# Two hybrid transformer blocks: in both token mixers each engine takes its work in an order of its own

## The chip, the cores and the metric

The kernel is one launch on one core of a Trainium2 chip. The metric is device time in microseconds (us) of that launch, as the median of three runs, on which nothing of the host counts. Engines are named as in the profile: PE (TensorE, matmuls), DVE (VectorE), ACT (ScalarE), POOL (GpSimd), SP (SyncE, which only issues the transfers of the weights).

## The reference

Two blocks of two layers each run one after the other on x of 256 tokens by 1024 features, in fp32.

```python
def first_block(x, c, ...):                       # twice
    mod = (silu(c) @ ada_w[l] + ada_b[l]).reshape(b_, 3, 3, D_MODEL)
    y = swiglu(modulate(x, ...), ffn_w13[l, 0], ffn_w2[l, 0])      # 1024 -> 2*2816 -> 1024
    x = layer_norm(ALPHA * x + 0.5 * (1 + gate) * y, ...)
    y = token_mixer(modulate(x, ...), w_in[l], w_out[l], ...)
    x = layer_norm(ALPHA * x + (1 + gate) * y, ...)
    y = swiglu(modulate(x, ...), ffn_w13[l, 1], ffn_w2[l, 1])
    x = layer_norm(ALPHA * x + 0.5 * (1 + gate) * y, ...)

def token_mixer(h, w_in, w_out, ...):
    # h @ w_in, then three kinds of heads of 64 features, then @ w_out
    oa = gated_delta_rule(l2norm(q), l2norm(k), v, g, beta)        # 6 heads, chunks of 64
    oa = oa * rsqrt(mean(oa * oa) + eps) * gdn_norm * silu(z)
    ob = moba_attention(q, k, v)                                   # 4 heads
    hc = mlstm_chunkwise(q, k, v, i_pre, logf)                     # 6 heads
    hc = (hc*sigmoid(o) - mean) * rsqrt(var + eps) * mlstm_norm
    return concatenate([oa, ob, hc]) @ w_out

def hybrid_layer(x, mem, ...):                    # the second block, twice
    proj = x @ w_in                                                # 4608 columns
    da_o = rms_norm(diff_attention(dq, dk, dv, lam)) * (1 - lam_init)
    hg_o = rms_norm(hgrn2_chunk_scan(forward) + hgrn2_chunk_scan(backward)) * silu(gate)
    mx_o = memory_attention(q, mem @ w_mem_kv)
    x = layer_norm(ALPHA * x + concatenate([da_o, hg_o, mx_o]) @ w_out)
    u = conv3(x @ w_up); x = layer_norm(ALPHA * x + (silu(gate) * val) @ w_down)
```

## The kernel before

**Stages.** The work runs as stages one after the other: per layer of the first block a gated feed-forward, mixer 1, a second feed-forward; per layer of the second block mixer 2 and a feed-forward with a convolution. Each stage multiplies the activations by weights that stream once from memory.

**Weights.** A matrix comes in chunks of 128 x 2048 fp32. SP issues a chunk's transfer into a ring of four buffers W. ACT casts it to the high part h (`Feed.hi`, L564), DVE subtracts to get the low part l (`Feed.lo`, L579), each into one of three buffers. A chunk's cast waits until PE has done with the matrix three before it (`released`). The same call of `Feed.lo` also does pending sums for the modulation vectors (L596). An fp32 product is three matmuls: h times high, l times high, h times low.

**Tiles.** In a mixer PE goes through 32 (mixer 1) or 36 (mixer 2) tiles. A tile is 24 matmuls (L683 to L685, or L696 to L698) into one of two banks in turn. Tile t therefore waits until tile t-2 has been emptied, by ACT (L2176 and near it; L3042 to L3062) or DVE (the causal convolution of mixer 1, L2236).

**Tasks.** Beside the tiles the mixers have tasks, each written for each engine as a generator that yields after a piece. Mixer 1: r (rows of gates and norms, 8 pieces), g (gated delta rule, 49), b (MoBA, 10), m (mLSTM, 13). In g the pieces 17 to 40 are six levels of a triangular inverse by doubling; in each PE multiplies (L1657, L1659: product U; L1675, L1677: product V), ACT copies U (L1855, L1857), DVE subtracts V (L1795). Pieces 41 to 45 form u and the output, 46 to 48 the norm (squares on ACT L1876, sums L1812 on DVE, the root on POOL L1903, products L1816 and L1820), 49 the transposes on PE (L1565) with the split into high and low parts (ACT L1573, DVE L1581 and L1583). m7 is the output product of mLSTM (L2033, L2034), m8 to m12 its norm, m13 its transposes. b10 is MoBA's last split (L1982). Mixer 2: h (HGRN, 43 pieces; h10, 14, 18, 22, 26, 30 and 31 are the products of its levels, L2379, before them the exponentials on ACT, L2610, products on DVE and repeated rows on POOL), d (diff attention, 17; d17 the transposes), e (memory attention, 6; on PE scores L2915, transposes L2924, sums L2932).

**Closing chunks.** The output projection takes 128x512 matmuls (L711 to L713). A first part of it is placed among the last pieces: `out(c)`, 24 matmuls each, two in mixer 1 and four in mixer 2. The rest, the tail, follows them all. In mixer 2 the first two closing chunks read the output of d, the other two that of h, the tail that of e. In mixer 1 the first two read g, the tail the rest.

**What sets the order.** There is one list for each mixer (ORDER1, ORDER2), made from AFTER and AFTER2: after tile n come the pieces named there. PE, DVE and ACT all play that list (`play1`, `play2`). The next chunk's cast and subtraction have no entry: they are done inside `tile`, at the first tile of a chunk, and inside `out`. POOL and SP have their own fixed code. Each engine does its instructions strictly in its order; semaphores make one wait for another.

Of the kernel before, what the change touches and what calls it, by code (L numbers as in the profile page):

```python
# [2323 lines left out]

AFTER2 = ["", "", "", "", "h", "h", "h", "", "h", "h", "h", "hh", "hh", "hh", "hh", "hh", "hh", "hh", "hh", "hhd", "hhd", "hh", "hhd", "hd",
          "hd", "hd", "h", "hd", "hd", "hd", "hd", "hd", "hd", "d", "hd", "hd"]


def order2():
    out = []  # L2330
    for t in range(36):
        out.append(("tile", MIX2[t // 2], t % 2))
        out += [(x,) for x in AFTER2[t]]
    out += [("e",), ("d",), ("e",), ("d",), ("h",), ("e",), ("out", 0), ("e",), ("out", 1), ("e",), ("out", 2), ("e",), ("out", 3)]
    return out


ORDER2 = order2()


def play2(tile, out, **tasks):
    for x in ORDER2:
        if x[0] == "tile":
            tile(x[1], x[2])
        elif x[0] == "out":
            out(x[1])
        else:
            next(tasks[x[0]], None)
    for t in tasks.values():
        for _ in t:  # L2350
            assert False

# [724 lines left out]
def dve_mix2(k, v, s, feed):  # L3077
    l = STAGES[s][1]
    cs = downs(s)
    bounds = dve_bounds(k, v)  # L3080

    def tile(n, j):
        m = FIRST["win2", l, n]
        feed.lo(m + 1 + j)

    def out(c):
        feed.lo(cs[c] + 2)
        if l == 0 and c in (1, 2):
# [144 lines left out]
```

## Time and profile before

| | us |
|---|---|
| median of three runs | 2339.38 (2336.34 to 2340.5) |
| the profiled execution's own time | 2344.83 |
| its span in the profile | 2343.0 |
| PE busy in the span | 2096.9 (89%) |
| DVE, ACT, POOL busy | 1642.7 (70%), 1090.5 (47%), 329.3 (14%) |

The profiled execution is 5.45 us above the median of the runs. The page gives the granted clock of TensorE too, in tenths of full speed: it is 9 or more nearly all along, with some slices of 8 where a mixer ends. The mean is 0.943. Mixer 1 of layer 0 lies at 286 to 560 us, mixer 2 of its layer 0 at 1410 to 1690, mixer 2 of layer 1 at 1893 to 2140; each stretch holds the layer norm at its end.

### The profile page before, as it was taken

Reading aid. Unit: us, or ns where it says so; the run is one execution under the profiler, and the core shown is the slowest. Engines: PE = TensorE matmul, PEld = TensorE weight load, DVE = VectorE, ACT = ScalarE, POOL = GpSimd, SP = SyncE. Lnnn points to the kernel's source line nnn. Section 1 sums busy time; section 2 is a strip of 40 time slices with the busy share of each in tenths; the row PEclk is TensorE's granted clock in tenths of the full one; section 3 lists DMA queues with packets and bytes.
Section 4 is the critical chain, followed back from the end, with each engine's and each line's share of the span. In section 5 each row is a group of like instructions: output and inputs, shape, how many; then the busy total and the mean of one; then the engine's idle time right before and its main releaser. Section 6 shows DMA issues by size and latency. Waiting matters only on the chain.

```text
span 2343.0 us, 35483 instructions
## 1 busy us (share of the span) xinstructions
PE 2096.9 (89%) x14804; PEld 1944.4 (83%) x14804; DVE 1642.7 (70%) x2189; ACT 1090.5 (47%) x1543; POOL 329.3 (14%) x261
## 2 busy tenths in 40 slices
PE   6999889978999999889979996887899988978998
PEld 6999778877997998778969985886799887967996
DVE  6777777548777866776557556975688579657874
ACT  3443463434433543553345434654556465545652
POOL 0000113103000200303012002710110036002000
PEclk9999999989999999999989997998999989978999
DMA  9877642114777667432125653332344543313552
GB/s 365 326 273 303 224 165 107 42 67 181 285 286 283 226 251 276 162 135 85 58 93 189 226 205 138 135 108 73 114 174 182 200 144 125 111 70 144 180 186 102
DMA packets 59791, 409.97 MB, mean 175 GB/s; under 512 B 6832, under 2 KB 6832, under 8 KB 12912
## 3 DMA queue, kind: packets, MB, share of 16 engines
q1 hardware_dynamic: 53424, 384.85, 44.3%
q0 software_dynamic: 5920, 22.43, 2.5%
q8 instruction: 118, 1.93, 0.3%
q10 hardware_dynamic: 288, 0.42, 0.0%
q14 instruction: 41, 0.34, 0.0%
HBM read 404.53 MB, written 3.15 MB: 174 GB/s over the span
## 4 chain that ended last, share of the span: by engine, by line
PE 68%; DVE 20%; ACT 6%; issue 3%; DMA 2%; POOL 2%; DVEq 0%; POOLq 0%; SPq 0%; ACTq 0%
PE ps L683 12%; PE ps L685 11%; PE ps L684 11%; PE ps L711 6%; PE ps L713 6%; PE ps L712 6%; DVE l L579 6%; PE ps L1677 2%; PE ps L696 2%; ACT h L564 2%; PE ps L698 1%; PE ps L697 1%; PE ps L1659 1%; DVE acc L596 1%; DVE gq L2236 1%
## 5 line engine op out<-in xcount | busy, mean ns | idle before, releaser
L579 DVE TENSOR_TENSOR l<-w,h 128x2048 fp32r<-128x2048 f32 (+1 forms) x296 | 689.8, 2334 | 230.7 <-ACT h L564 230.1
L683 PE MATMUL ps<-xh,h 128*128 128x256 f32 x2688 | 780.5, 290 | 50.6 <-DVE xl L862 8.5
L684 PE MATMUL ps<-xl,h 128*128 128x256 f32 x2688 | 765.8, 285 | 0.0
L685 PE MATMUL ps<-xh,l 128*128 128x256 f32 x2688 | 765.3, 285 | 0.0
L564 ACT CAST h<-w 128x2048 fp32r<-128x2048 f32 (+1 forms) x296 | 558.6, 1893 | 302.8 <-PE ps L713 157.1
L683 PEld LDWEIGHTS ps<-xh,h 128*128 128x128 f32 x2688 | 521.3, 194 | 68.9 <-issue 26.6
L684 PEld LDWEIGHTS ps<-xl,h 128*128 128x128 f32 x2688 | 521.1, 194 | 1.9 <-issue 1.9
L685 PEld LDWEIGHTS ps<-xh,l 128*128 128x128 f32 x2688 | 520.9, 194 | 0.0
L711 PE MATMUL ps<-h,hh 128*128 128x512 f32 x528 | 207.2, 392 | 0.0
L713 PE MATMUL ps<-h,hl 128*128 128x512 f32 x528 | 205.5, 389 | 0.0
L712 PE MATMUL ps<-l,hh 128*128 128x512 f32 x528 | 205.4, 389 | 0.0
L904 POOL DMA_DIRECT2D GB<-in_vec x20 | 11.4, 572 | 1176.0 <-DVE ab L806 570.7
L596 DVE SCALAR_TENSOR_TENSOR acc<-w,sc,acc 128x1024 f32<-128x1024 f32 x126 | 167.7, 1331 | 2.8
L696 PE MATMUL ps<-h,xh 128*128 128x256 f32 (+1 forms) x512 | 152.5, 298 | 7.6 <-ACT dqk L3048 6.5
L697 PE MATMUL ps<-l,xh 128*128 128x256 f32 (+1 forms) x512 | 146.5, 286 | 0.0
L698 PE MATMUL ps<-h,xl 128*128 128x256 f32 (+1 forms) x512 | 146.3, 286 | 0.0
L1116 DVE TENSOR_TENSOR hl<-hf,hh 128x256 fp32r<-128x256 f32 x132 | 69.6, 529 | 82.4 <-ACT hh L1111 81.9
L713 PEld LDWEIGHTS ps<-h,hl 128*128 128x128 f32 x528 | 99.1, 188 | 20.8
L712 PEld LDWEIGHTS ps<-l,hh 128*128 128x128 f32 x528 | 99.2, 188 | 20.6 <-issue 0.5
L711 PEld LDWEIGHTS ps<-h,hh 128*128 128x128 f32 x528 | 99.2, 188 | 20.4 <-issue 0.5
L696 PEld LDWEIGHTS ps<-h,xh 128*128 128x128 f32 x512 | 101.4, 198 | 14.7 <-issue 11.6
L697 PEld LDWEIGHTS ps<-l,xh 128*128 128x128 f32 x512 | 101.3, 198 | 0.0
(412 smaller groups left out, 3061.6 us busy)
## 6 DMA issues: line engine op xcount, KB each, us to landing
w<-in_stream SPq DMA_DIRECT2D x362, 1024.0 KB, 4.9
GB<-in_vec POOLq DMA_DIRECT2D x20, 512.0 KB, 6.0
gate<-in_vec POOLq DMA_DIRECT2D x6, 512.0 KB, 4.1
w<-in_stream SPq DMA_DIRECT2D x6, 512.0 KB, 3.8
cst<-in_cst POOLq DMA_DIRECT2D x1, 1160.0 KB, 16.1
memf<-in_memT SPq DMA_DIRECT2D x1, 1024.0 KB, 8.5
xf<-in_xT POOLq DMA_DIRECT2D x1, 1024.0 KB, 9.7
kv<-mk POOLq DMA_DIRECT2D x2, 512.0 KB, 7.1
```

Source lines behind the costliest of these rows:

```text
L564: e.copy(k.H[m % NH][:, 0:z], k.W[n % NW][:, 0:z]).then_inc(k.hi_done, 1)
L579: e.tensor_tensor(k.L[m % NH][:, 0:z], k.W[n % NW][:, 0:z], k.H[m % NH][:, 0:z], SUB).then_inc(k.lo_done, 1)
L596: e.scalar_tensor_tensor(out=A[:, :], in0=W[:, i, :], scalar=k.SC[:, r:r + 1], in1=A[:, :], op0=MUL, op1=ADD).then_inc(k.ada_sum, 1)
L683: p.matmul(P[:, 0:T], H[:, r, o], xh[:, r, :], start=r == 0, stop=False)
L684: p.matmul(P[:, 0:T], H[:, r, o], xl[:, r, :], start=False, stop=False)
L685: i = p.matmul(P[:, 0:T], L[:, r, o], xh[:, r, :], start=False, stop=r == 7)
L696: p.matmul(P[:, 0:n], xh[:, r, o], H[:, r, :], start=r == 0, stop=False)
L697: p.matmul(P[:, 0:n], xh[:, r, o], L[:, r, :], start=False, stop=False)
L698: i = p.matmul(P[:, 0:n], xl[:, r, o], H[:, r, :], start=False, stop=r == 7)
L711: p.matmul(P[:, :], hh[:, f, o], H[:, i, s], start=b, stop=False)
L712: p.matmul(P[:, :], hh[:, f, o], L[:, i, s], start=False, stop=False)
L713: x = p.matmul(P[:, :], hl[:, f, o], H[:, i, s], start=False, stop=e)
```

## The change

The two lists and the functions that played them go. In their place stand six strings, one for each of PE, DVE and ACT in each mixer. A letter is an entry: t a tile, r g b m and h d e the next piece of that task, o a closing chunk (PE only), w one call for the next chunk (`feed.hi` on ACT, `feed.lo` on DVE). The number of pieces, tiles and chunks is what it was. So the cast and the subtraction of a chunk no longer belong to a tile. Two bookkeeping pieces of block 2 (`act_bounds`, `dve_bounds`) go with the chunks that they went with. On DVE of mixer 2, t does nothing. The wait of the gated delta rule's first piece on PE becomes that for both halves of the gate rows, where it was for one. ACT has 2 table loads fewer (41 for 43), one in front of L1541 in each mixer 1. All other instructions are the same, and POOL's and SP's order is unchanged.

Cut to its core (the strings of one mixer; two of the functions that play them):

```diff
-AFTER = ["r", "r", "r", "r", "rr", "r", "r", "g", "g", "gg", "", "gg", "g", "gb", "ggb", "ggb", "ggb", "ggb", "gggb", "gggb", "gggb", "ggb",
-         "gggm", "ggm", "gggm", "ggm", "gggm", "ggm", "gm", "gm", "gm", "gm"]
...
-def play1(tile, out, **tasks):
-    for x in ORDER1:
-        if x[0] == "tile":
-            tile(x[1], x[2])
-        elif x[0] == "out":
-            out(x[1])
-        else:
-            next(tasks[x[0]], None)
+ORDER1 = dict(
+    pe=("t t t t trrrrrrr t tg trg tg t t tg tgggg t t tgbbgg tggb tbgbgg tgggb t tbggggg tgggggg tbbm tmg tm tggggggggg tm tgmg tg tg "
+        "tmg tgmgggoommbmmmm"),
...
+def interleave(order, **parts):
+
+    for x in order.replace(" ", ""):
+        if x in parts:
+            next(parts[x])
...
+def more(f, feed, n):
+
+    for _ in range(n):
+        f(feed.m)
+        yield
...
-    yield from pe_decays(k, p, l, 0, lambda g: GBANK["dk", g], gp, gv, ga, k.rv(l, "RB"))
+    yield from pe_decays(k, p, l, 0, lambda g: GBANK["dk", g], gp, gv, ga, k.rv(l, "RB", 1))
...
     def tile(n, j):
         m = FIRST["win", l, n]
-        if j == 0:
-            feed.hi(m + 2)
...
-        if j == 0:
-            feed.lo(m + 1)
...
-        if j == 0:
-            feed.lo(m + 2)
...
-    play2(tile, out, h=dve_hgrn(k, v, l), d=dve_diff(k, v, l), e=dve_memory(k, v, l))
+    interleave(ORDER2["dve"], w=more(ahead, feed, ORDER2["dve"].count("w")), h=dve_hgrn(k, v, l), d=dve_diff(k, v, l), e=dve_memory(k, v, l))
```

**DVE, end of mixer 1, layer 0, before.** `hc`, `s`, `msq` belong to m, `os`, `ms`, `zs` to g, `l` is a chunk's low part.

```order
L579 TENSOR_TENSOR l_22_70<-w_16_64,h_19_67 128x2048
L2080 TENSOR_TENSOR hc_142<-hc_142,so_106 128x384 x2
L2083 TENSOR_REDUCE s_115<-hc_142 128x6 x2
L2086 TENSOR_SCALAR s_115<-s_115 128x6 x2
L2089 TENSOR_TENSOR hc_142<-hc_142,s_115 128x384 x2
L1812 TENSOR_REDUCE ms_113<-gsq_137 128x6 x2
L2094 TENSOR_REDUCE s_115<-msq_143 128x6 x2
L1816 TENSOR_TENSOR os_136<-os_136,ms_113 128x384 x2
L1820 TENSOR_TENSOR os_136<-os_136,zs_105 128x384 x2
L1982 TENSOR_TENSOR mixl_74<-mo_111,mixh_73 128x256 x2
L2098 TENSOR_TENSOR hc_142<-hc_142,s_115 128x384 x2
```

The same place after:

```order
L579 TENSOR_TENSOR l_22_70<-w_16_64,h_19_67 128x2048
L2060 SCALAR_TENSOR_TENSOR Dk_92_140<-ps,Dk_92_140 128x384 x2
L1819 TENSOR_REDUCE ms_113<-gsq_137 128x6 x2
L1823 TENSOR_TENSOR os_136<-os_136,ms_113 128x384 x2
L1827 TENSOR_TENSOR os_136<-os_136,zs_105 128x384 x2
L1588 TENSOR_SCALAR gtmp_139<-ps,cols_50 128x256
L1590 TENSOR_TENSOR mixl_74<-gtmp_139,mixh_73 128x256
L1588 TENSOR_SCALAR gtmp_139<-ps,cols_50 128x256
L1590 TENSOR_TENSOR mixl_74<-gtmp_139,mixh_73 128x256
L1588 TENSOR_SCALAR gtmp_139<-ps,cols_50 128x256
L1590 TENSOR_TENSOR mixl_74<-gtmp_139,mixh_73 128x256
L2069 TENSOR_SCALAR s_115<-ps 128x6 x2
```

The norm of g (now L1819 to L1827) and its splits stand in one run, and m's come behind them; before, m's first steps stood ahead of g's and the two were mixed. The split of b10 (L1982) has gone further back.

In the same mixer PE's string has `tggggggggg` for tile 26: the nine pieces g32 to g40, products V of the fourth level to V of the sixth, stand with no tile between them. Before, they stood in groups of one to three with tiles 24 to 27 between them.

**ACT, start of mixer 2, layer 0, before.** `K` are HGRN's gates, `qs` its queries, `h` a chunk's high part.

```order
L3044 COPY K_97_145<-ps 128x256
L564 CAST h_18_66<-w_16_64 128x2048
L3044 COPY K_97_145<-ps 128x256 x2
L3059 ACT_TABLE_LOAD
L3059 ACTIVATE K_97_145<-K_97_145 128x1024
L564 CAST h_19_67<-w_13_61 128x2048
L3042 COPY qs_144<-ps 128x256
```

After:

```order
L564 CAST h_18_66<-w_16_64 128x2048
L3028 COPY K_97_145<-ps 128x256 x2
L3043 ACT_TABLE_LOAD
L3043 ACTIVATE K_97_145<-K_97_145 128x1024
L564 CAST h_19_67<-w_13_61 128x2048
L564 CAST h_17_65<-w_14_62 128x2048
L3026 COPY qs_144<-ps 128x256 x2
```

A chunk's cast moved ahead of the copies that empty two tiles, and two casts (for the 5th and 6th w of the mixer) now stand one behind the other before the next copy.

**PE, end of mixer 2, layer 0, before.** `epp`, `epT`, `xq`, `mk`, `mmv` belong to e, `do` to d, `ho` to h; L711 begins the first closing chunk.

```order
L2915 MATMUL ps<-mk_176,xq_151 128x256 x2
L2924 MATMUL ps<-cst_49,epp_178 128x128 x4
L2915 MATMUL ps<-mk_176,xq_151 128x256 x2
L1565 MATMUL ps<-cst_49,do_173 128x128 x8
L1565 MATMUL ps<-cst_49,ho_186 128x128 x8
L2932 MATMUL ps<-epT_179,mmv_177 128x256 x2
L2924 MATMUL ps<-cst_49,epp_178 128x128 x4
L2915 MATMUL ps<-mk_176,xq_151 128x256 x2
L711 MATMUL ps<-h_19_67,mixh_119_167 128x512
```

The same place after:

```order
L2901 MATMUL ps<-mk_176,xq_151 128x256 x2
L1572 MATMUL ps<-cst_49,do_173 128x128 x8
L1572 MATMUL ps<-cst_49,ho_186 128x128 x8
L711 MATMUL ps<-h_19_67,mixh_119_167 128x512
L712 MATMUL ps<-l_22_70,mixh_119_167 128x512
L713 MATMUL ps<-h_19_67,mixl_120_168 128x512
```

PE behind the fourth closing chunk of that mixer, after, up to the tail (L711):

```order
L2918 MATMUL ps<-epT_179,mmv_177 128x256 x2
L2910 MATMUL ps<-cst_49,epp_178 128x128 x4
L2901 MATMUL ps<-mk_176,xq_151 128x256 x2
L2918 MATMUL ps<-epT_179,mmv_177 128x256 x2
L2910 MATMUL ps<-cst_49,epp_178 128x128 x4
L2918 MATMUL ps<-epT_179,mmv_177 128x256 x2
L711 MATMUL ps<-h_17_65,mixh_119_167 128x512
```

The transposes of e (now L2910) no longer stand ahead of those of d and h (now L1572); three pieces of e come together behind the last closing chunk, where before each had a closing chunk behind it.

## Rows read from the trace of the kernel before

**Rows 1.** Windows: stretch, length, PE, PEld, DVE, ACT, POOL busy, PEclk, DMA share, GB/s.

```profile
286.00:560.00 274.00, 234.50 (x1724) 215.19 (x1723) 179.76 (x320) 119.81 (x201) 51.69 (x47) 0.93 0.28 101
...
1410.00:1690.00 280.00, 224.30 (x1509) 203.09 (x1508) 202.07 (x310) 147.32 (x245) 72.08 (x56) 0.88 0.32 114
1893.00:2140.00 247.00, 210.06 (x1452) 192.06 (x1451) 176.95 (x252) 134.93 (x213) 64.98 (x44) 0.90 0.31 112
```

**Rows 2.** Windows over the end of mixer 1 and of mixer 2, layer 0.

```profile
504.00:532.00 28.00, 17.13 (x64) 13.29 (x65) 15.54 (x26) 11.30 (x18) 5.54 (x4) 0.76 0.13 40
1613.00:1669.00 56.00, 41.50 (x164) 31.28 (x164) 32.01 (x73) 21.08 (x43) 2.11 (x3) 0.79 0.22 77
```

**Rows 3.** Waits of PE, 286 to 562: us in total, times, longest.

```profile
PE ps L1565 <- DVE os L1820: 8.9, 1, 8.9
...
PE ps L683 <- DVE gq L2236: 2.4, 3, 1.5
PE ps L1554 <- DVE AT L1752: 2.2, 1, 2.2
PE ps L1599 <- ACT rs L1834: 2.2, 1, 2.2
...
PE ps L1675 <- ACT Ub L1857: 1.7, 1, 1.7
```

**Rows 4.** DVE lines by form, 370 to 470: busy, mean ns, idle before.

```profile
L1795 DVE TENSOR_TENSOR Xb<-Xb,ps 128x384 f32<-128x384 f32 x20 | 10.9, 547 | 2.4 <-PE ps L1677 1.9
```

**Rows 5.** Timeline at the end of mixer 1: start us, us, instruction, [idle before].

```profile
485.77 1.50 PE L2034 MATMUL ps<-vx,Dk 128*128 128x65 f32 x12
...
489.57 0.39 PE L2034 MATMUL ps<-vx,Dk 128*128 128x65 f32 x2
...
500.92 0.48 ACT L1872 COPY os<-ps 128x384 f32<-128x384 f32 x1 [2.20 <-PE ps L1717]
...
504.10 1.28 ACT L2209 ACT_TABLE_LOAD   x1
...
506.68 1.01 DVE L1812 TENSOR_REDUCE ms<-gsq 128x6 f32<-128x384 f32 x2 [3.82 <-ACT gsq L1876]
...
508.08 2.31 POOL L1903 TENSOR_TENSOR ms<-ms,cst 128x12 f32<-128x12 f32 x1
...
512.54 1.09 PE L1565 MATMUL ps<-cst,os 128*128 128x128 f32 x4 [8.86 <-DVE os L1820]
...
531.18 0.39 PE L711 MATMUL ps<-h,mixh 128*128 128x512 f32 x1
```

**Rows 6.** Waits of PE, 1410 to 1690.

```profile
PE ps L2924 <- DVE epp L2957: 8.6, 3, 7.2
PE ps L2379 <- DVE A L2496: 6.7, 3, 5.0
```

**Rows 7.** Timeline of ACT at the start of mixer 2.

```profile
1462.09 0.39 ACT L3046 ACTIVATE K<-ps 128x256 f32<-128x256 f32 x1 [2.44 <-PE ps L685]
1462.37 1.91 ACT L564 CAST h<-w 128x2048 fp32r<-128x2048 f32 x1
1464.92 0.37 ACT L3044 COPY K<-ps 128x256 f32<-128x256 f32 x1 [0.64 <-PE ps L685]
```

**Rows 8.** DVE and POOL lines by form, 1498 to 1526.

```profile
L579 DVE TENSOR_TENSOR l<-w,h 128x2048 fp32r<-128x2048 f32 x4 | 12.1, 3019 | 0.0
...
L2672 POOL TENSOR_TENSOR E<-B 128x512 f32<-128x512 f32 x7 | 16.8, 2397 | 4.3 <-DVE QL L2554 4.3
```

**Rows 9.** The page, costliest groups: busy, mean ns.

```profile
L579 DVE TENSOR_TENSOR l<-w,h 128x2048 fp32r<-128x2048 f32 (+1 forms) x296 | 689.8, 2334 | 230.7 <-ACT h L564 230.1
```

**Rows 10.** Timeline at the end of mixer 2, layer 0.

```profile
1621.96 1.09 PE L2924 MATMUL ps<-cst,epp 128*128 128x128 f32 x4 [7.18 <-DVE epp L2957]
...
1626.79 1.11 PE L1565 MATMUL ps<-cst,do 128*128 128x128 f32 x4 [2.04 <-ACT epp L2767]
...
1668.52 0.40 PE L711 MATMUL ps<-h,mixh 128*128 128x512 f32 x1
```

More of the change, by code:

```diff
@@ L2149, in out @@
         pe_down_one(k, pe, c, keys, banks, k.mixh1, k.mixl1, ready)
-    play1(tile, out, r=pe_rows(k, p, l), g=pe_gdn(k, p, l), m=pe_mlstm(k, p, l), b=pe_moba(k, p, l))
+    interleave(ORDER1["pe"], t=each(tile, tiles1(l)), o=each(out, [(0,), (1,)]), r=pe_rows(k, p, l), g=pe_gdn(k, p, l), m=pe_mlstm(k, p, l),
+         b=pe_moba(k, p, l))
     pe_down_tail(k, pe, s, keys, banks, k.mixh1, k.mixl1, ready)
@@ L2209, in tile @@
             e.activation(k.zs[:, :, :], k.zs[:, :, :], ACT.Silu).then_inc(out, 1)
-    play1(tile, lambda c: feed.hi(cs[c] + 2), r=act_rows(k, e, l), g=act_gdn(k, e, l), m=act_mlstm(k, e, l), b=act_moba(k, e, l))
+    interleave(ORDER1["act"], t=each(tile, tiles1(l)), w=more(feed.hi, feed, ORDER1["act"].count("w")), r=act_rows(k, e, l), g=act_gdn(k, e, l),
+         m=act_mlstm(k, e, l), b=act_moba(k, e, l))
     feed.hi(cs[-2] + 2)
@@ L2322, in mixer2_steps @@
             k.ea.add(l, **step("h", c), **step("p", b), **step("e", a, 2))
[L2325 to L2351, printed above, removed]
+ORDER2 = dict(
+    pe=("th t t t t thh t t t thh thh t t t thhhhhhhhh thhhh t tdhh th thdh t thhhhd td tdh thh td t thhd thdhh thd thdh thhd td tdd t "
+        "tddedhoeoeooeee"),
+    dve=("t t wwwh t wt thh t wh wt t wth t t t t th whhhhhhh t wthhhh thhh wt th wdhhd thh wh thhh td wthdhdh wdh th td t wh thhd tdh "
+        "wtd t th wt thd t t whdh wddded tdh we we wweee"),
+    act=("wt wt t t wt th wt t wwth thh t t wt thhhhhhhhh whhhh t t wh thh wth thd t whh tdd t wdhhhh th wh td thh t wh tdhd whh t thh "
+        "tddd t whh whhd td t wtdddd t tedh wwee wweee"),
+)
+TILES2 = [(c, j) for c in MIX2 for j in range(2)]
 def wide(x):
@@ L3024, in out @@
         pe_down_one(k, pe, c, keys, banks, k.mixh2, k.mixl2, ready)
-    play2(tile, out, h=pe_hgrn(k, p, l), d=pe_diff(k, p, l), e=pe_memory(k, p, l))
+    interleave(ORDER2["pe"], t=each(tile, TILES2), o=each(out, [(c,) for c in range(4)]), h=pe_hgrn(k, p, l), d=pe_diff(k, p, l), e=pe_memory(k, p, l))
     pe_down_tail(k, pe, s, keys, banks, k.mixh2, k.mixl2, ready)
@@ L3034, in tile @@
         m = FIRST["win2", l, n]
-        if j == 0:
-            feed.hi(m + 2)
         t = TILE[m] + j
@@ L3065, in tile, with ahead @@
             e.activation(k.hgate[:, :, :], k.hgate[:, :, :], ACT.Silu).then_inc(o, 1)
-    def out(c):
-        feed.hi(cs[c] + 2)
-        if l == 0 and c == 1:
+    def ahead(m):
+        feed.hi(m)
+        if l == 0 and m == cs[1] + 2:
             act_bounds(k, e)
-    play2(tile, out, h=act_hgrn(k, e, l), d=act_diff(k, e, l), e=act_memory(k, e, l))
+    interleave(ORDER2["act"], t=each(tile, TILES2), w=more(ahead, feed, ORDER2["act"].count("w")), h=act_hgrn(k, e, l), d=act_diff(k, e, l), e=act_memory(k, e, l))
     feed.hi(cs[-2] + 2)
@@ L3080, in dve_mix2, with ahead @@
     bounds = dve_bounds(k, v)
[L3082 to L3088, printed above, removed]
+    def ahead(m):
+        feed.lo(m)
+        if l == 0 and m in (cs[1] + 2, cs[2] + 2):
             next(bounds)
-    play2(tile, out, h=dve_hgrn(k, v, l), d=dve_diff(k, v, l), e=dve_memory(k, v, l))
+    interleave(ORDER2["dve"], w=more(ahead, feed, ORDER2["dve"].count("w")), h=dve_hgrn(k, v, l), d=dve_diff(k, v, l), e=dve_memory(k, v, l))
     feed.lo(cs[-2] + 2)
```

26 lines of the change are left out of this document (14 added, 12 removed).

## The prediction

> **What bounds the kernel now.** I read the page's busy line first: PE works 89% of the span, so PE's instructions are the floor, and a new order can only win what PE idles or runs slowly. Then windows over the mixers, since only they change: mixer 1 has PE busy 234.5 of 274 us at a granted clock of 0.93, mixer 2 224.3 of 280 at 0.88 in its layer 0 and 210.1 of 247 at 0.90 in its layer 1 [rows 1]. So 39.5, 55.7 and 36.9 us are idle. The lower clock is a second loss: over 280 us, 0.88 in place of 1 is up to 34 us of work not done. Most of both lies at the ends: 504 to 532 has PE busy 17.1 of 28 at 0.76, 1613 to 1669 41.5 of 56 at 0.79 [rows 2]. Third, PE's waits. In mixer 1 one wait of 8.9 stands out, for DVE's product `os`; then 2.4 for the convolution `gq`, 2.2 for `AT`, 2.2 for `rs`, 1.7 for `Ub` [rows 3]. In mixer 2 it is 8.6 for `epp` and 6.7 for `A`, HGRN's levels [rows 6]. Last, the timelines at the ends [rows 5, 10], for what each late result had in front of it.
>
> No instruction is dropped but two table loads of 1.28 each [rows 5], on ACT, which is idle most of the time there. I cost them at nothing. All else is position. I take each mixer in turn and read the second layer as the first.
>
> **Mixer 1, early part.** DVE now takes a tile's convolution ahead of the chunk's subtraction (its string has `t t wtrr`), so a tile's bank comes free up to one subtraction, 2.3 [rows 9], earlier. The three waits for `gq`, 2.4 together, go. The wait for `rs` (2.2) stands where r's pieces alternate with tiles; ACT and PE now take r in a block, with tiles ready ahead. The wait for `AT` (2.2) goes, as g's scores come a tile later on PE [rows 3]. Together 6.8; the clock is low for a while behind each, which I count with no more than 0.2: -7. Bounds: 0, where each wait comes back at the next piece in the same chain, and -10, where the clock gives half as much again.
>
> **Mixer 1, levels.** PE now plays nine pieces of the inverse in a row behind tile 26. Each level needs DVE's subtractions of the product V, 547 ns each [rows 4], eight to a level, 4.4 in all, between a V and the next. Tiles covered that before. PE's own 24 matmuls of a level cover about half. By my timeline, with a chunk's subtraction (2.3) also in DVE's string there, PE idles 5.2 in two or three waits, in place of the 1.7 for `Ub` [rows 3]: +3.5. Bounds: 0, where the subtraction falls between, and +8, where the 2.3 and a half clock behind each wait come on top.
>
> **Mixer 1, end.** Let X be 500.9, when ACT copies g's output. Before, ACT did a table load and silu ahead of g's squares (504.1 to 506.1), DVE summed at 506.7, POOL took 2.3 for the root, DVE's two products followed, and PE transposed at 512.5 = X+11.6 after the wait of 8.9; the tail began at 531.2 = X+30.3 [rows 5]. Now squares come first on ACT, DVE has nothing in between, and PE has m7 behind the last tile to fill the time: 24 matmuls, 485.8 to 490.0, 4.2 [rows 5]. X itself comes 4.2 sooner, since m7 was ahead of it. From X: copies and squares 1.0 + 0.9, sums 1.0, POOL 0.2 + 2.3, products 2.0, with starts and overlaps X+7.8 for the transposes. What then is last is m's chain on DVE, which is now wholly behind g's: g's splits till X+10.6, denominators and products 3.4, gate and mean 3.3, squares on ACT 1.0, sums 1.0, POOL 2.5, product 1.0, a subtraction of a chunk 2.3, transposes and splits 2.2: X+27.3. So the tail starts 4.2 + 3.0 = 7.2 sooner, and two closing chunks run at a better clock, which is inside that bound. I take -7. Bounds: 0, if m's chain is longer by what g's was shortened; and -15.6, the wait of 8.9 and the clock of the 28 us, 28 x 0.24 = 6.7 [rows 2].
>
> Mixer 1: -7 + 3.5 - 7 = -10.5 each, -21 for two layers.
>
> **Mixer 2, start and levels.** ACT copies a tile in 0.4 and casts in 1.9, and a tile takes PE 2.8 (the two copies stand 2.83 apart) [rows 7]. Where ACT's string has `wwt`, two casts stand ahead of a tile's copy: 3.8 against 2.8, and the second also waits for a buffer that PE frees. PE then waits about 2.4 at the 11th tile. The levels' chain starts 4.5 to 6.8 later than before, while the waits of before for `A` (6.7) [rows 6] shrink as tiles stand between the levels. Played through, both orders stand at 1557 by tile 25. I take 0, bounds -6 and +8 per layer: below, all of the 6.7; above, the later start plus the 2.4 uncovered.
>
> In 1498 to 1526 the chunk's subtractions took 3.02 on the mean against 2.33 over the kernel, while POOL repeated rows, seven at 2.4 [rows 8, 9]. The Trainium skill (SBUF — State Buffer, "Who interferes with whom") has VectorE and GpSimd share a port pair under a lock held for a whole instruction, so that one waits for the other. The trace agrees. By that rule a subtraction moved into or out of these 28 us costs or gives 0.7; the strings leave about one fewer there, so the sum would be about 1 us lower, and it does not speak against the change.
>
> **Mixer 2, end.** Before, PE's transposes of e's second piece stood ahead of d's: they waited 7.2 (8.6 with two others [rows 6]) till 1622.0, d's transposes came at 1626.8, and the tail began at 1668.5 [rows 10]. PE stood from 1614.8 (1622.0 less 7.2) with d's transposes behind the wait. My timeline has them at 1618.2, as e's exponentials no longer hold DVE, and the first closing chunk at 1625.8. The four chunks then have no e between them but e2 and e3. The price: e4, e5 and e6 stand bare before the tail, and each is scores, exponentials, transposes, sums through three engines. My timeline starts the tail at 1661.4: -7. Bounds: -15 (the waits of 7.2 and 2.0 in front of d gone, and the clock of 0.79 back at 0.9: 56 x 0.11 = 6 [rows 2]), and +3 (e's last three chains bare, each 3 to 4 us longer than a covered one, against 7 saved).
>
> Mixer 2: 0 - 7 each, -14 for two layers.
>
> **Sum.** -21 - 14 = -35. The profiled execution's own time is 2344.8, so 2309.8; it lies 5.45 above the median, so the forecast in the median's terms is 2304.
>
> **Rivals.** B, the new order hides the levels as well. For it: mixer 1's waits between `AT` and the end are few and short [rows 3], so tiles cover much. Against: nine pieces bare. Then mixer 1 is -14 each, and mixer 2 gets 6.7 for `A` besides its 7: 2 x (-14 - 13.5) = -55, 2284.
>
> C, the ends win and the starts lose. Against the forecast speaks that each early wait is short and may come back at the next piece. Mixer 1's early part is half (-7 each layer together instead of -10.5), mixer 2's start costs +8 against its end's 7: -14 + 2 = -12, 2327.
>
> D, slower, by mixer 2's levels. Each of HGRN's seven products needs an exponential on ACT. If in ACT's new string it stands behind a cast and a copy that wait for PE, each level is later by 1.9 + 0.4 = 2.3 [rows 7], 16 in a layer. Up to about 8 are hidden, by the same playing through, since the chain ends that long before its transposes are due; beyond, it pushes d's and h's transposes and takes the end's gain too. That is +15 a layer with nothing of the -7: -21 + 30 = +9, 2348. For it: the clusters `ww` and `www` on ACT and DVE. Against: they stand mostly where no level is due.
>
> E, nothing changes: the waits turn up elsewhere for the same sum, since PE's 89% and DVE's subtractions bound both: 2339.
>
> **How the numbers follow.** Forecast 0.53 (2304), B 0.17 (2284), C 0.12 (2327), D 0.13 (2348), E 0.05 (2339). What a measurement can tell from no change is about 0.2%, 4.7 us. The forecast, B and C are faster by more, 0.80 with what their lower ends leave; D is slower, 0.14 with E's upper side; same 0.06. The range leaves out D, E and the lower part of B: 2281 to 2337.
>
> **What would show it.** Right: PE's wait for `os` at mixer 1's end under 2 us; m7 between the last tile and the transposes; the tail's first matmul some 27 us behind g's output; new waits for `Xb`, `XT` or `Ub` in the block of nine; in mixer 2 no `epp` wait ahead of d's transposes, but waits for it behind the fourth closing chunk; clock in the end windows at 0.85 or more. Wrong: d's or h's transposes later than before against the last tile (D); waits for `A` longer than 6.7 in all, or gone (D, B); the tail of mixer 1 at the same distance from the last tile with waits in m's norm in place of g's.

## The result and the profile after

The changed kernel takes 2243.9 us, median of 4 runs (2243.28 to 2244.2); before, on the same chip, 2337.86 (2335.72 to 2340.5). The ratio is 0.9597, 95% interval 0.9585 to 0.9609: 94 us faster, where 35 were forecast, and below the range. The profiled execution's own time is 2243.28, its span 2241.5. In the two traces the difference is 101.5 us (spans of 2343.0 and 2241.5), since the profiled execution of before lies above its median; the sums below go by the traces.

I split each mixer at PE's last tile. The length of a mixer is from its first tile to the first matmul of the layer norm behind it (L779); "before the last tile" is from the first tile's first matmul to the last one's end.

| us against before, layer 0 / 1 | forecast | measured |
|---|---|---|
| mixer 1 before the last tile, less the 4.2 of m7 that moved behind it | -3.5 | -25.0 / -26.3 |
| mixer 1 behind it, with m7 | -7 | -7.9 / -7.9 |
| mixer 2 before the last tile | 0 | -9.7 / -7.8 |
| mixer 2 behind it | -7 | -8.1 / -6.4 |
| all other stages together | 0 | -2.4 |

Behind the last tile the sizes are near the forecast. What I had nearly at nothing before the last tile gave 69 of the 99 us that the mixers are shorter. Windows over just these stretches, mixer 1 of layer 0 and mixer 2 of layers 0 and 1, of before (columns as in [rows 1]):

```profile
282.60:503.70 221.10, 198.91 (x1558) 186.62 (x1558) 144.29 (x261) 95.39 (x156) 42.22 (x35) 0.95 0.28 100
1448.40:1613.10 164.70, 150.17 (x1200) 145.45 (x1200) 131.08 (x162) 99.61 (x148) 61.94 (x35) 0.94 0.35 123
1891.80:2060.70 168.90, 150.75 (x1200) 145.95 (x1200) 133.46 (x170) 99.73 (x148) 60.14 (x35) 0.93 0.33 120
```

The same, after:

```profile
281.70:473.60 191.90, 184.56 (x1525) 176.50 (x1525) 144.32 (x245) 93.94 (x158) 43.72 (x37) 0.97 0.32 116
1381.40:1536.40 155.00, 145.11 (x1200) 140.98 (x1200) 133.20 (x168) 98.72 (x148) 62.34 (x37) 0.97 0.37 132
1806.10:1967.20 161.10, 148.31 (x1200) 144.48 (x1200) 135.31 (x176) 98.64 (x148) 58.38 (x37) 0.94 0.36 127
```

In mixer 1 PE idles 7.3 in place of 22.2 us, which is 14.9. Its busy time falls by 14.4, of which m7 is 4.2 (36 matmuls, where the prediction says 24; three of them still start inside the window after, hence 1558 and 1525). The other 10 are the same matmuls, done faster. In mixer 2, with the same 1200 matmuls, it is 4.6 of idle time and 5.1 of busy time in layer 0, 5.4 and 2.4 in layer 1. So with each microsecond of PE's waits that went, half a microsecond to a little over one of busy time went too.

The granted clock gives most of that, not all. Each window's length times what its clock lacks to 1 is the work lost to the clock: 221.1 x 0.05 = 11.1 before and 191.9 x 0.03 = 5.8 after in mixer 1, so 5.3 of the 10; the same sum gives 5.2 of the 5.1 and 2.2 of the 2.4 in mixer 2. Where the other 5 of mixer 1 come from is not shown. The low clock stands behind waits: behind the 1.7 for `Ub` [rows 3], at 469.4, it is 0.50 for 6.8 us.

```profile
470.00:476.80 6.80, 6.80 (x34) 6.46 (x33) 1.81 (x4) 0.00 (x0) 0.00 (x0) 0.50 0.06 22
```

PE's waits in mixer 1 after, 280 to 527, what stands in place of [rows 3]:

```profile
PE ps L683 <- ACT A L1470: 4.1, 1, 4.1
PE ps L1572 <- DVE mtmp L1588: 1.9, 1, 1.9
...
PE ps L683 <- DVE gq L2241: 1.5, 2, 1.0
PE ps L1572 <- DVE hc L2105: 1.3, 1, 1.3
...
PE ps L1572 <- DVE os L1827: 0.3, 1, 0.3
```

Neither `rs`, `AT`, `Xb` nor `Ub` is left. Of before, [rows 3] leave out these, among others:

```profile
PE ps L1659 <- DVE Xb L1795: 2.1, 1, 2.1
...
PE ps L1632 <- DVE Xb L1768: 1.6, 1, 1.6
PE ps L683 <- ACT mv L2189: 1.1, 1, 1.1
```

Up to and with the wait for `AT` PE's waits fall by 7.4, where I forecast 6.8. Behind it, in the levels, 7.8 us of waits stood before (`Xb` 2.1 and 1.6, `Ub` 1.7, the gate 0.8 and 0.6, `Dk` 0.6, `vb` 0.4), and 0.4 is left, where I forecast 3.5 more.

The block of nine pieces, where I expected 5.2 of new waits, has none: a window over it and tile 26 shows PE busy all of its 16 us at full clock. A level's 24 matmuls for U take 2.84 in it, its 48 for V 5.5 (435.0 to 440.5).

```profile
427.00:443.00 16.00, 16.00 (x166) 15.88 (x166) 11.62 (x21) 6.97 (x16) 0.00 (x0) 1.00 0.25 97
```

```profile
432.34 2.84 PE L1666 MATMUL ps<-Xb,Al 128*128 128x128 f32 x24
```

The end of mixer 1 after, which answers to [rows 5]:

```profile
470.80 0.48 ACT L1879 COPY os<-ps 128x384 f32<-128x384 f32 x1 [2.20 <-PE ps L1724]
471.44 0.95 ACT L1883 ACTIVATE gsq<-os 128x384 f32<-128x384 f32 x2
472.01 1.01 DVE L1819 TENSOR_REDUCE ms<-gsq 128x6 f32<-128x384 f32 x2 [4.68 <-ACT gsq L1883]
...
473.40 1.45 PE L2041 MATMUL ps<-vx,Dk 128*128 128x65 f32 x12
...
477.86 0.63 PE L1572 MATMUL ps<-cst,os 128*128 128x128 f32 x4 [0.33 <-DVE os L1827]
...
496.87 0.78 PE L711 MATMUL ps<-h,mixh 128*128 128x512 f32 x1
```

g's transposes come 7.1 behind ACT's copy (7.8 forecast, 11.6 before) with m7 (L2041) in the gap, and the tail 26.1 behind it (27.3 forecast, 30.3 before). In front of the tail PE now waits 1.3 and 1.9 for m's `hc` and `mtmp`. In mixer 2, PE's waits after, 1343 to 1605, in place of [rows 6]:

```profile
PE ps L2365 <- DVE A L2482: 5.6, 2, 3.1
...
PE ps L1572 <- ACT epp L2753: 3.4, 1, 3.4
PE ps L683 <- ACT qs L3026: 2.4, 1, 2.4
```

Before, two more stood there that [rows 6] leave out; the second is gone, of the first 0.8 is left:

```profile
PE ps L696 <- ACT dqk L3048: 3.2, 1, 3.2
...
PE ps L2705 <- ACT pp L2767: 2.7, 1, 2.7
```

The end of mixer 2 after, in place of [rows 10]:

```profile
1541.41 1.12 PE L1572 MATMUL ps<-cst,do 128*128 128x128 f32 x4 [3.38 <-ACT epp L2753]
...
1579.67 1.13 PE L2918 MATMUL ps<-epT,mmv 128*128 128x256 f32 x4 [1.31 <-DVE mixl L2947]
1581.34 0.63 PE L2910 MATMUL ps<-cst,epp 128*128 128x128 f32 x4 [0.54 <-ACT mixh L2973]
1582.74 1.10 PE L2918 MATMUL ps<-epT,mmv 128*128 128x256 f32 x4 [0.77 <-ACT epT L2969]
```

d's transposes stand 5.0 behind the last tile (13.7 before, 5.1 by my timeline). The wait of 7.2 for e's `epp` (L2957) in front of them is gone, but 3.4 for ACT's `epp` of L2753 stand there, where 2.0 stood before. The wait for `qs` is 2.4, as worked out. The last pieces of e stand bare; their waits are short, yet from the first closing chunk to the layer norm it is 44.8 us, where it was 39.0. The windows over the two ends, in place of [rows 2]:

```profile
474.00:502.00 28.00, 23.59 (x108) 18.88 (x108) 21.54 (x45) 11.83 (x15) 6.17 (x3) 0.88 0.22 75
1536.00:1590.00 54.00, 44.52 (x192) 34.42 (x191) 31.67 (x73) 22.76 (x43) 3.26 (x5) 0.91 0.27 97
```

**What I had not looked at** is what stands in front of a late result on the engine that makes it. In mixer 1 of before it is often a step for the next chunk. Here DVE's subtraction of a chunk (L579) stands ahead of `AT` and of `Xb`, with no idle time between, while PE waits:

```profile
359.53 2.28 DVE L579 TENSOR_TENSOR l<-w,h 128x2048 fp32r<-128x2048 f32 x1
...
361.73 1.94 DVE L1752 TENSOR_TENSOR AT<-ps,Dk 128x384 f32<-128x384 f32 x4
...
362.33 1.17 PE L1554 MATMUL ps<-kb,gq 64*128 64x128 f32 x10 [2.23 <-DVE AT L1752]
...
424.82 2.28 DVE L579 TENSOR_TENSOR l<-w,h 128x2048 fp32r<-128x2048 f32 x1
427.02 0.55 DVE L1795 TENSOR_TENSOR Xb<-Xb,ps 128x384 f32<-128x384 f32 x1
...
427.62 4.22 PE L1659 MATMUL ps<-Xb,Al 128*128 128x128 f32 x24 [2.10 <-DVE Xb L1795]
```

The wait of 1.6 for `Xb` at 377.8 has a subtraction of 1.2 and two sums of 2.6 together in front of it. In the same way ACT's cast of 1.9 stands right ahead of the copies `mv` (PE waits 1.1) and, in mixer 2, `dqk` (3.2); there DVE's subtraction also stands right ahead of each of the three `A` that PE waits for (6.7). And ahead of `rs`, for which PE waits 2.2, ACT has one of the two table loads that the change drops:

```profile
335.09 1.28 ACT L1541 ACT_TABLE_LOAD   x1
```

The second thing is what DVE itself waits for. Its line for the chunks, 282 to 505 of before, and 281 to 475 after (busy, mean ns, idle before):

```profile
L579 DVE TENSOR_TENSOR l<-w,h 128x2048 fp32r<-128x2048 f32 (+1 forms) x18 | 39.5, 2198 | 20.5 <-ACT h L564 20.5
```

```profile
L579 DVE TENSOR_TENSOR l<-w,h 128x2048 fp32r<-128x2048 f32 (+1 forms) x18 | 39.7, 2212 | 2.4 <-ACT h L564 2.4
```

Before, DVE stood 20.5 us in mixer 1 at a chunk's subtraction for ACT's cast; after it is 2.4. Over the whole kernel the idle time in front of that line was 230.7 in [rows 9], a row that I used for its mean alone; after it is 159.4. In before, though, little of this idle time is what PE waited for: of its six stretches in mixer 1 (8.0, 5.9, 4.7, 1.3 and two under half a microsecond) only the 1.3 at 373.5 stands directly ahead of something that PE waits for, the `Xb` of 377.8. Ahead of `AT` and the other `Xb` the subtraction has its cast in time, and its busy time is what holds them up. Whether the rest of the 20.5 cost PE anything in before is not shown.

### The profile page after: what moved, and what is told of

Same layout as the page of the kernel before. It is cut to its first block, busy times and chain, and to the rows that moved or that the text cites. A ratio compares the mean times of both kernels' runs of the same rounds, so it can differ in the third digit from the quotient of the medians.

```text
span 2241.5 us, 35481 instructions
## 1 busy us (share of the span) xinstructions
PE 2063.7 (92%) x14804; PEld 1923.6 (86%) x14804; DVE 1641.3 (73%) x2189; ACT 1084.2 (48%) x1541; POOL 330.3 (15%) x261
## 4 chain that ended last, share of the span: by engine, by line
PE 76%; DVE 15%; ACT 4%; issue 2%; POOL 2%; DMA 1%; POOLq 0%; DVEq 0%; SPq 0%; ACTq 0%
PE ps L683 14%; PE ps L684 13%; PE ps L685 13%; PE ps L711 6%; PE ps L713 6%; PE ps L712 6%; DVE l L579 3%; PE ps L696 2%; PE ps L1684 2%; PE ps L697 2%; PE ps L698 2%; DVE acc L596 1%; PE ps L1666 1%; PE ps L1561 1%; PE ps L614 1%
## 5 line engine op out<-in xcount | busy, mean ns | idle before, releaser
L579 DVE TENSOR_TENSOR l<-w,h 128x2048 fp32r<-128x2048 f32 (+1 forms) x296 | 688.8, 2331 | 159.4 <-ACT h L564 159.0
L711 PE MATMUL ps<-h,hh 128*128 128x512 f32 x528 | 207.2, 392 | 0.0
L696 PE MATMUL ps<-h,xh 128*128 128x256 f32 (+1 forms) x512 | 147.6, 288 | 1.8 <-ACT dqk L3032 0.8
L711 PEld LDWEIGHTS ps<-h,hh 128*128 128x128 f32 x528 | 99.1, 188 | 20.5 <-issue 0.5
L1130 ACT ACTIVATE sa<-ps 128x256 f32<-128x256 f32 x88 | 33.8, 385 | 143.1 <-PE ps L685 143.1
```

The costliest lines, as they stand in the source:

```text
L579: e.tensor_tensor(k.L[m % NH][:, 0:z], k.W[n % NW][:, 0:z], k.H[m % NH][:, 0:z], SUB).then_inc(k.lo_done, 1)
L696: p.matmul(P[:, 0:n], xh[:, r, o], H[:, r, :], start=r == 0, stop=False)
L711: p.matmul(P[:, :], hh[:, f, o], H[:, i, s], start=b, stop=False)
```

## The experiments

All are the changed kernel with other strings. The strings can also spell the common order of before (in `ends_new`, every engine has before's instructions in before's order up to the cut), so that old and new can be mixed along a mixer, in this way for each of the three engines (the runs' kernels hold the strings that come of it):

```python
def cut(a, b, n):   # order a up to tile n with the pieces behind it, then b
    ...             # without what a has already played (counted letter by letter)
```

No run gives one engine alone its old or new string over a whole mixer, so what each engine's order gives by itself is open. The table has the mixers' lengths against before, from each run's one trace, and DVE's wait for casts (L579) before the last tile in layer 0. The ratios are to runs of before beside each group, whose medians were 2337.7 to 2340.8. Where two runs have the same strings in a mixer, its lengths agree within 0.7 us (`block_wtw` and `cast_apart` in mixer 2).

| kernel | median us | ratio to before (95%) | mixer 1, layer 0 / 1 | mixer 2, layer 0 / 1 | DVE's wait for casts, mixer 1 / 2 |
|---|---|---|---|---|---|
| before | | | 259.5 / 259.5 | 229.9 / 233.4 | 20.5 / 12.5 |
| after | 2243.90 | 0.9597 (0.9585 to 0.9609) | -32.9 / -34.2 | -17.8 / -14.2 | 2.4 / 5.6 |
| ends_old | 2269.03 | 0.9686 (0.9670 to 0.9702) | -23.2 / -27.4 | -12.5 / -10.5 | 7.1 / 5.6 |
| ends_new | 2320.76 | 0.9911 (0.9896 to 0.9926) | -9.9 / -7.0 | -2.4 / -3.8 | 16.2 / 12.7 |
| front12 | 2342.37 | 1.0001 (0.9989 to 1.0014) | -4.9 / -4.8 | +3.7 / +4.4 | 13.9 / 12.9 |
| front20 | 2301.02 | 0.9827 (0.9807 to 0.9847) | -14.2 / -11.1 | -7.2 / -7.9 | 7.7 / 12.8 |
| block_wtw | 2256.63 | 0.9641 (0.9627 to 0.9656) | -25.9 / -25.4 | -17.1 / -17.5 | 2.4 / 4.5 |
| w_old | 2328.79 | 0.9949 (0.9932 to 0.9965) | -15.6 / -17.2 | +11.0 / +7.4 | 22.7 / 12.0 |
| w_new | 2362.06 | 1.0090 (1.0075 to 1.0105) | -8.9 / -8.7 | +20.8 / +16.4 | 9.4 / 23.9 |
| end_e | 2244.08 | 0.9590 (0.9572 to 0.9608) | -33.3 / -33.1 | -13.8 / -17.2 | 2.3 / 5.8 |
| one_cast | 2260.16 | 0.9664 (0.9646 to 0.9683) | -25.7 / -26.4 | -15.7 / -14.0 | 9.8 / 5.6 |
| one_swap | 2268.07 | 0.9697 (0.9678 to 0.9715) | -30.1 / -31.7 | -6.2 / -6.4 | 4.8 / 18.9 |
| m7_back | 2248.07 | 0.9611 (0.9592 to 0.9630) | -31.0 / -31.0 | -18.0 / -14.5 | 2.4 / 5.6 |
| cast_apart | 2237.80 | 0.9577 (0.9556 to 0.9597) | -32.8 / -34.1 | -17.8 / -17.6 | 2.4 / 5.3 |

**Where along the mixers.** `ends_old` and its complement:

```diff
-ORDER1 = new; ORDER2 = new
+ORDER1 = cut(new, old, 28); ORDER2 = cut(new, old, 35)   # ends_old
+ORDER1 = cut(old, new, 28); ORDER2 = cut(old, new, 35)   # ends_new
```

> New order in mixer 1 up to tile 28 and in mixer 2 up to tile 35, the common order of before behind. Theory M (the work before the last tile gives most: PE's short waits and the low clock behind them go): mixer 1 keeps 25 of its 33 to 34 us, mixer 2 keeps 8 to 10 of 14 to 18, total about 2274. Rival N (the ends give it, what shows ahead of them is only work moved behind): mixer 1 keeps under 12, mixer 2 under 3, total above 2305.

> The complement: the common order of before up to tile 28 in mixer 1 and tile 35 in mixer 2, the new order only behind. Theory M: about -8 us per mixer 1 and -7 per mixer 2, total about 2308. Rival N: -20 or more per mixer 1, total below 2290.

Theory M holds: with the old ends mixer 1 keeps 23 and 27 us, mixer 2 12.5 and 10.5; with the new ends alone it is 10 and 7, and 2.4 and 3.8, for mixer 2 half of what I expected. By both runs the ends are worth 7 to 10 us in mixer 1 and 2 to 5 in mixer 2. In `ends_old` the wait for `os` is the 8.9 of [rows 3] again:

```profile
PE ps L1569 <- DVE os L1824: 8.9, 1, 8.9
```

```diff
+ORDER1 = cut(new, old, 12); ORDER2 = cut(new, old, 14)   # front12
+ORDER1 = cut(new, old, 20); ORDER2 = cut(new, old, 24)   # front20
```

> New order only up to tile 12 of mixer 1 and tile 14 of mixer 2, then the order of before. Theory M, gain spread evenly: -6 to -9 us per mixer 1, 0 to -3 per mixer 2, total 2315 to 2325. Rival F (one place in front, the block of r, gives most of mixer 1): -15 or more per mixer 1, total below 2305.

> New order up to tile 20 of mixer 1 and tile 24 of mixer 2, then the order of before. Theory M, gain spread evenly: -12 to -16 us per mixer 1, -4 to -7 per mixer 2, total 2290 to 2305. Rival F: no more than what the first 12 and 14 tiles gave.

Mixer 1's gain is spread: about 5 by tile 12, 11 to 14 by tile 20, 23 to 27 by tile 28. No single place gives it (rival F falls; `front12` missed its -6 by one, and with mixer 2 its total). In mixer 2 the first 14 tiles cost 4, where 0 to -3 was expected: the start's loss that my rival C had. Tiles 15 to 24 give 11 to 12. In `front12` the gain of mixer 1 and the loss of mixer 2 make no difference in the whole kernel (1.0001), so the total alone hides both.

**Chunks or pieces.** In `w_old` ACT's casts of mixer 1 and all of mixer 2's casts and subtractions stand at their tiles as before, while the pieces keep the new order; the start of one string shows it. `w_new` is the reverse; in it mixer 1 has DVE's subtractions moved, not ACT's casts. The pieces' order takes in the ends, which are new in `w_old` and old in `w_new`.

```diff
 # mixer 1, act, from the start (w_old)
-t wt wrrrr t wt t wt wrrr t trg t wgg
+wt wt rrrr t wt t wt rrr t wt rg wt gg
```

> The changed kernel's pieces and tiles, but chunks at their tile again: on ACT in mixer 1, on ACT and DVE in mixer 2. If freeing the chunks from the tiles is what gives the gain before the last tile, mixer 1 loses 10 us or more of its 33 and mixer 2 all of its 8 to 10 there; if the order of the pieces gives it, under 3 in each mixer: total below 2256.

> The reverse: pieces and tiles in the common order of before, and only the chunks at the places that the changed kernel gives them among the tiles: on DVE in mixer 1, on ACT and DVE in mixer 2. If the chunks give the gain, mixer 1 -10 or more and mixer 2 -8; if the pieces give it, within 2 us of before in each mixer: total 2335 to 2345.

For `w_old` the first half of the expectation holds: mixer 1 loses 17 of its 33 and mixer 2 ends 7 to 11 behind before. For `w_new` neither half holds: mixer 1 gains 9, and mixer 2 doesn't gain what `w_old` loses there, it loses 16 to 21. So chunks and pieces are not two gains that add; a cast's place is good or bad for one order of pieces. In mixer 2, layer 0, PE waits 14.8 us for chunks' low parts `l` in `w_old` and 12.2 for `A`. In `w_new` it waits 13.7 for ACT's copies `qs` and `K` (1.8 before) and 12.6 for `A` (6.7), and DVE's wait for casts is 23.9 where it was 12.5; one of the waits for `A`, of 5.1, stands behind such a wait of 4.6. DVE's wait for casts isn't the whole of it: in mixer 1 `w_old` has 22.7, no less than before, and is still 16 us shorter.

**One letter.** In mixer 1 ACT's cast of one chunk goes behind the next three pieces, where `w_old` had it. In `one_swap` DVE's subtraction of that chunk goes back as well, behind g, b and a tile, with which the product for the gate comes (L633).

```diff
 # mixer 1, act (one_cast and one_swap)
-tgg wggb tg tg wb
+tgg ggbw tg tg wb
 # mixer 1, dve (one_swap)
-tgggg t wgb tggggg
+tgggg t gb tw ggggg
 # mixer 2, pe (one_cast)
-thhhhhhhhh thhhh t
+thhhhh thhhhhhhh t
```

> The changed kernel with one letter of ACT's string for mixer 1 moved three pieces back, the cast of the chunk that w 12 brings, to where the common order had it. Theory H (DVE stands at a chunk's subtraction until ACT's cast, and what PE waits for stands behind it): DVE waits about 7 us at that subtraction, PE about 6 behind it, and the low clock adds 1 to 3: mixer 1 +7 to +9 each. Rival S (a single cast has slack, only the pieces' order counts): 0 to 1. In mixer 2 PE's block h8 to h16 is parted by tile 16 after five pieces: 0 if such blocks are free, 2 to 7 slower if, as in mixer 1, tiles are worth more later.

> As one_cast in mixer 1, and DVE's subtraction of that chunk moved three letters back too, behind the gate's product. Theory H: PE's wait of 6 us goes, since the gate is no longer behind the late cast: most of the loss comes back, mixer 1 within 3 us of the changed kernel. If the late cast itself is what costs (PE waits for the chunk's low part), mixer 1 stays at +7 to +9. In mixer 2 ACT's casts stand at their tiles as before and DVE's subtractions where the changed kernel has them: by theory H +10 or more each, as DVE then waits for casts there.

Theory H's numbers come out: mixer 1 is 7.2 and 7.8 longer for one letter. The 7 and 6 us of waits in the expectation are those that the trace of `w_old` has in this place; what the run adds is that this one cast alone brings them. The timeline of `one_cast` in that place:

```profile
395.25 1.50 PE L1663 MATMUL ps<-Xb,Al 128*128 128x128 f32 x12
...
396.12 0.48 ACT L1859 COPY Ub<-ps 128x384 f32<-128x384 f32 x1 [9.09 <-PE ps L1663]
...
397.16 0.87 ACT L2001 COPY bS<-ps 128x384 f32<-128x384 f32 x2
397.91 1.92 ACT L564 CAST h<-w 128x2048 fp32r<-128x2048 f32 x1
...
399.86 2.29 DVE L579 TENSOR_TENSOR l<-w,h 128x2048 fp32r<-128x2048 f32 x1 [7.39 <-ACT h L564]
402.07 0.68 DVE L633 TENSOR_TENSOR gate<-ps,gate 128x512 f32<-128x512 f32 x1
...
402.81 2.93 PE L1663 MATMUL ps<-Xb,Al 128*128 128x128 f32 x12 [6.05 <-DVE gate L633]
```

Read it backwards: PE can't go on with U (L1663) until DVE has read the gate's bank; DVE stands 7.39 at the subtraction; the cast stands on ACT behind copies of U that wait 9.09 for PE. Three engines wait round a chain in which nobody has much to do. Behind the wait 12 matmuls take 2.93 where the 12 ahead of it took 1.50; the granted clock is 0.50 there:

```profile
401.10:407.90 6.80, 5.09 (x24) 5.10 (x25) 2.63 (x4) 2.61 (x4) 2.00 (x2) 0.50 0.45 154
```

With the swap, DVE's wait for casts falls to 4.8, PE's wait of 6.05 goes, and mixer 1 is within 2.8 and 2.5 us of the changed kernel. The first waits of DVE in mixer 1, `one_cast` and then `one_swap`:

```profile
DVE l L579 <- ACT h L564: 9.8, 3, 7.4
```

```profile
DVE l L579 <- ACT h L564: 4.8, 3, 2.4
```

In mixer 2 `one_swap` has only ACT's casts at the old places: +11.6 and +7.8 against the changed kernel, with DVE's wait for casts at 18.9 (5.6): H again, a little under its +10 in layer 1. PE's waits for `A` are 13.7 in layer 0 (5.6); one of 7.0 stands behind a wait of DVE for a cast of 6.3. Parting PE's block h8 to h16 in `one_cast` cost 2.1 in layer 0 and nothing in layer 1.

**The block of nine, and two small edits.**

```diff
 # mixer 1, pe (block_wtw)
-tm tggggggggg tm tgmg tg tg
+tm tggg tggg tggg mgmg tg tg
 # mixer 2, act (block_wtw, cast_apart)
-tt wwth thh
+tt wtwh thh
```

> The changed kernel with two edits. Mixer 1, PE: the nine pieces behind tile 26 stand three by three with tiles 27 and 28 between. If the block costs what my prediction gave it (5.2 us of new waits for 1.7 old), each mixer 1 gets 2 to 3.5 us shorter; if it is free, as its trace has no wait in it, 0 or up to 2 longer. Mixer 2, ACT: the first cast pair w w t becomes w t w. If the pair makes PE's wait for qs (2.4), each mixer 2 gets about 2.4 shorter; if that wait has been covered by later waits on the chain of HGRN's levels, 0. Total 2243.9 less 0 to 11.

Parting the block makes mixer 1 7.0 and 8.8 longer, the opposite sign to my step and more than the rival's 2. Two new waits of PE, 440 to 461, and a low clock behind them:

```profile
PE ps L1691 <- ACT gq L2166: 2.1, 1, 2.1
PE ps L696 <- DVE gq L2238: 1.2, 1, 1.2
```

```profile
441.00:451.00 10.00, 8.76 (x98) 8.31 (x96) 4.97 (x12) 3.41 (x6) 0.00 (x0) 1.00 0.01 2
451.00:461.00 10.00, 7.87 (x40) 7.30 (x39) 3.89 (x5) 3.65 (x5) 0.00 (x0) 0.67 0.27 96
```

In the changed kernel's timeline a tile stands on PE while ACT makes `gq` (447.7 to 450.6); in `block_wtw` the two tiles are spent among the nine pieces and PE has none left there. Of the 7 us in layer 0, 3.6 are idle time of PE; the other 3.4 are busy time, with the clock at 0.67 in that window.

> The changed kernel with ACT's first pair of casts in mixer 2 parted by a tile (w t w for w w t). In block_wtw this stood at +0.7 in layer 0 and -3.3 in layer 1. If the pair's wait for qs counts, -1 to -3 each: total 2238 to 2242, which would beat the changed kernel; if later waits take it up, 2243 to 2245.

The edit gives +0.1 in layer 0 and -3.4 in layer 1, as in `block_wtw` (-3.3). The median is 2237.8, the ratio 0.9577 against the changed kernel's 0.9597, and the intervals overlap. It is the best time measured, but the totals don't tell it apart; what speaks for it is layer 1 in two traces. In layer 0 the wait for `qs` shrinks too (2.4 to 0.4), and the waits for `A` grow from 5.6 to 7.4 in its place. In layer 1 the wait for `qs` (2.4) goes and those for `A` fall from 7.1 to 6.1.

```diff
 # mixer 1, pe (m7_back)
-tmg tgmgggoomm
+tmg m tggggoomm
 # mixer 1, pe (end_e)
-tggggggggg tm tgmg
+tggggg tgggg m tgmg
 # mixer 2, pe / dve / act (end_e)
-hoeoeooeee / hwewewweee / hwweewweee
+hoeoeoeoee / hwewewewee / hwewewewee
```

> The changed kernel with m's output product m7 ahead of the last tile again on PE of mixer 1, as before. My prediction's term: the start of g's chain on ACT and DVE slips by the 4.2 us of those matmuls, and PE stands idle in their place: +4 each mixer 1, plus 1 to 2 for the clock. If m7 was no more than moved work, 0.

It costs 2.0 and 3.2: the sign and the place are right (PE's wait for `os` is 3.8 in place of 0.3), the size is under the 4 that I gave, and further under the 5 to 6 with the clock. What takes up the rest isn't shown.

> The changed kernel with e's pieces between the closing chunks at the end of mixer 2 on all three engines (o e o e o e o e e on PE in place of o e o e o o e e e). If the bare e pieces behind the fourth closing chunk are what gives back 6 to 7 us there, each mixer 2 gets 3 to 6 shorter; if the time from the first closing chunk to the layer norm is set by DVE's chain whatever stands on PE, under 1. In mixer 1 the block of nine is parted once, by tile 27 after five: 0 to 1 either way.

Mixer 2 is 4.1 longer in layer 0 and 3.1 shorter in layer 1. The total is the changed kernel's. From the first closing chunk to the layer norm it is 48.7 and 44.3, where the changed kernel has 44.8 and 45.7. So this order isn't better; why it differs by layer stays open. In mixer 1 the block parted once, by one tile, costs nothing (-33.3 and -33.1 against -32.9 and -34.2), where `block_wtw` with two tiles cost 7.

## Why the prediction was wrong

**Right.** The end of mixer 1, in mechanism and size: m7 in the gap, the transposes 7.1 and the tail 26.1 behind ACT's copy; `ends_new` and `m7_back` bear out the place. The early part of mixer 1, in its waits (7.4 us gone, 6.8 forecast). In mixer 2's end the mechanism: d ahead of e, and the bare pieces of e that give back part. The start of mixer 2 does cost: PE's wait of 2.4 for `qs` is in the trace, and `front12` has +4.

**Right by luck in part: the size of mixer 2's end.** Behind the last tile mixer 2 gave 8.1 and 6.4, and 7 was forecast. But with the end's order of before it already gives 2.8 and 2.9 there (`ends_old`), so that part comes from the order ahead of it. The end's own order is worth 5.3 and 3.7 in company and 2.4 and 3.8 alone.

**Wrong, the step that failed:** "Mixer 1, levels", with its +3.5, and the 0 for mixer 2's "start and levels". Measured before the last tile, mixer 1 gave 25 and 26 where the early part and the levels were to give 3.5 together. Of the 21.5 us between forecast and layer 0, 11 are idle time in the levels (7.4 less in place of 3.5 more), and 10 are busy time of the same matmuls, which I had at no more than 0.2. I went from some of PE's waits one by one and asked whether each would go, and for the rest I kept what stood there. Three things failed in that:

- I counted eight subtractions of 547 ns [rows 4] as standing between one product and the next, half covered by "24 matmuls of a level". But a level of the block has 24 matmuls for U and 48 for V, 2.8 and 5.5 us, and DVE's subtractions follow PE six matmuls of V at a time, so that only the last one is left when V ends (in the block DVE starts it at 440.6). The block runs with no wait, and parting it by two tiles costs 7 to 9.
- I took 1.7 for `Ub` as all that the levels waited before, and so read the waits behind `AT` as "few and short". They were 7.8 us together. In mixer 2 I left out `dqk` (3.2) and `pp` (2.7).
- I never asked why these results were late. Before, a chunk's step stood directly ahead of several of them: of `AT`, both `Xb`, `mv` and, in mixer 2, `dqk` and `A`. Once chunks are free of the tiles, these steps can stand elsewhere. That a chunk's step in the wrong place costs this much is shown by `one_cast`: one cast three letters later makes a wait of 7.4 on DVE and costs 7 us, and moving the subtraction behind what PE needs gives 4 to 5 of them back. That it explains the whole gain is not shown: `w_old` moves back only ACT's casts in mixer 1 and loses half of its gain, and no run moves back the subtractions ahead of `AT` and `Xb` alone.

Rival B (the levels are hidden too, 2284) was worked out from the same rows, so it was too high as well.

**Mis-sized: the clock.** "The clock is low for a while behind each, which I count with no more than 0.2" for 6.8 us of waits. Busy time of the same matmuls before the last tile fell by 10 us in mixer 1, 5.1 and 2.4 in mixer 2: 10 against 14.9 us of waits gone, 5.1 against 4.6, 2.4 against 5.4. By the windows' mean clock 5.3, 5.2 and 2.2 of these are the clock. In `block_wtw` 3.6 us of new waits came with 3.4 of busy time in layer 0.

**Without weight.** The Trainium skill's rule on the shared port (SBUF — State Buffer, "Who interferes with whom") was to be worth about 1 us. Seven subtractions fall into the levels of mixer 2, layer 0, in both kernels (1489 to 1558 before, 1418 to 1485 after), so none was moved out; their mean is 2700 ns before and 2648 after, 0.4 us in all. That they are longer than the kernel's mean of 2331 beside POOL's work agrees with the rule.

**Not separated: the table load.** I cost the two table loads at nothing, since ACT is idle most of the time. But one of the two in before, 1.28 us, stood on ACT's chain to `rs`, for which PE waited 2.2. After, it and the wait are gone; how much of the wait was the load no run tells.

Of the rivals, C's loss at the start of mixer 2 exists and is outweighed behind it. D's mechanism, ACT's and DVE's clusters making HGRN's levels late, doesn't add to the waits for `A` with these strings (5.6 and 7.1 in the two layers, 6.7 and 8.0 before). In `w_new`, 16 to 21 us longer per mixer 2, it is there in part: 12.6 for `A`, beside 13.7 for ACT's copies.
